# Prompt attention by pairs of heads, with weights normalised by GpSimd ahead of their transposes

## What is computed

```
def _fox_block(q, cq, q_pos, k, v, ck, k_pos):        # 8 heads of 64, cq and ck cumulated log-forget gates
    s = jnp.einsum('bqhd,bkhd->bhqk', q, k) * (HEAD_DIM ** -0.5)
    s = s + cq[..., :, None] - ck[..., None, :]
    s = jnp.where(k_pos[None, :] <= q_pos[:, None], s, -jnp.inf)
    p = jax.nn.softmax(s, axis=-1)
    return jnp.einsum('bhqk,bkhd->bqhd', p, v)
merged = jnp.concatenate([_rmsnorm(y_ssm, g_ssm_out), _rmsnorm(o, g_attn_out)], axis=-1)
out = merged @ w_out
```

## Time and profile before

| | us |
|---|---|
| runs | 2373.78, 2384.41, 2386.98 (median 2384.41) |
| profiled execution | 2372.85, its span 2371.1 |
| prompt attention | 529.2 to 759.3 |
| sample sequences | to about 902 |
| output projection | 902.9 to 1040.4 |

### The profile page before, as it was taken

How to read it: one execution, slowest core, us unless ns; L and a number is a source line. 1 busy time by engine, 2 the same in 40 slices (tenths; PEclk the granted TensorE clock), 3 DMA queues, 4 the chain that set the end, 5 groups by cost and what they waited for, 6 DMA issues and landing times.

```text
span 2371.1 us, 28991 instructions
## 1 busy us (share of the span) xinstructions
PE 2078.4 (88%) x8262; PEld 1117.0 (47%) x8263; DVE 892.5 (38%) x2450; ACT 533.7 (23%) x993; POOL 300.3 (13%) x236
## 2 busy tenths in 40 slices
PE   4797899998888888978978999899899999998990
PEld 1456555446666334545434444444445455544450
DVE  2827400315554222234423333333333333333338
ACT  3423221015544112033111111111111111111122
POOL 0010100000000030000001122122122222221124
PEclk7898889999998998988988999999899999999995
DMA  9531200022000443001148899899888778898843
GB/s 335 218 155 23 113 0 1 0 76 58 18 1 18 131 138 133 0 19 58 52 176 279 288 298 293 277 295 297 265 273 250 250 241 259 266 288 281 287 102 137
DMA packets 100878, 394.20 MB, mean 166 GB/s; under 512 B 27279, under 2 KB 30003, under 8 KB 71996
## 3 DMA queue, kind: packets, MB, share of 16 engines
q1 hardware_dynamic: 70020, 302.44, 34.4%
q0 software_dynamic: 24768, 90.19, 15.9%
q10 hardware_dynamic: 6024, 0.73, 0.2%
HBM read 329.16 MB, written 62.57 MB: 165 GB/s over the span
## 4 chain that ended last, share of the span: by engine, by line
PE 27%; DMA 22%; issue 5%; SPq 4%; DVE 2%; ACT 1%; POOL 0%; POOLq 0%; DVEq 0%; ACTq 0%
DMA arena<-in_w_exp_down 22%; PE psum L961 11%; PE psum L989 5%; PE psum L830 5%; SPq L2209 2%; PE psum L947 1%; SPq L2204 1%; SPq L2205 1%; DVE arena L1607 1%; PE psum L858 1%; PE psum L864 1%; DVE arena L1617 1%; PE psum L871 0%; PE psum L809 0%; PE psum L854 0%
## 5 line engine op out<-in xcount | busy, mean ns | idle before, releaser
L961 PE MATMUL psum<-arena 128*128 x1360 | 631.1, 619 | 55.2 <-SPq L2230 51.5
L961 PEld LDWEIGHTS psum<-arena 128*128 128x128 f32 x1360 | 261.1, 197 | 358.3 <-issue 358.3
L989 PE MATMUL psum<-arena,tail 128*128 x672 | 302.3, 592 | 0.0
L2057 POOL DMA_INDIRECT moe_rows<-arena x84 | 133.4, 1588 | 815.2 <-ACT arena L1941 291.4
L1563 DVE TENSOR_TENSOR arena<-arena,psum 128x256 f32<-128x256 f32 x85 | 35.8, 421 | 499.2 <-ACT arena L1927 499.2
L989 PEld LDWEIGHTS psum<-arena,tail 128*128 128x128 f32 x672 | 121.1, 190 | 120.5 <-issue 120.5
L1927 ACT ACTIVATE arena<-psum 128x256 f32<-128x256 f32 x85 | 32.7, 385 | 644.3 <-PE psum L961 644.3
L678 PE MATMUL psum<-arena 128*128 128x512 f32 (+1 forms) x384 | 126.5, 493 | 0.0
L830 PE MATMUL psum<-arena 128*128 128x512 f32 (+1 forms) x288 | 124.3, 593 | 0.9 <-ACT arena L1853 0.5
L1541 DVE TENSOR_TENSOR arena<-tail,arena 128x1152 bf16<-128x1152 f32 x89 | 119.6, 1344 | 0.0
L1941 ACT ACTIVATE arena<-psum,arena 128x512 f32<-128x512 f32 x84 | 57.7, 687 | 213.3 <-PE psum L989 213.3
(11 more groups left out here) (486 smaller groups left out, 2342.1 us busy)
## 6 DMA issues: line engine op xcount, KB each, us to landing
arena<-in_w_exp_gate SPq DMA_DIRECT2D x64, 1024.0 KB, 5.3
arena<-in_w_exp_up SPq DMA_DIRECT2D x64, 1024.0 KB, 9.4
arena<-in_w_exp_down SPq DMA_DIRECT2D x64, 1024.0 KB, 12.3
arena<-in_w_ada SPq DMA_DIRECT2D x24, 1024.0 KB, 7.6
arena<-in_w_ada_final SPq DMA_DIRECT2D x8, 1024.0 KB, 6.5
arena<-in_cache_k SPq DMA_DIRECT2D x32, 256.0 KB, 3.4
arena<-in_cache_v SPq DMA_DIRECT2D x32, 256.0 KB, 2.9
arena<-in_w_in SPq DMA_DIRECT2D x1, 6176.0 KB, 18.5
```

The costliest lines, as they stand in the source:

```text
L961: ins = pe.matmul(slot[2 + par].rearrange("p (h n) -> p h n", h=2), xTs[:, par, k, :], ring_gu[:, at, :, k, :].rearrange("p a h n -> p (a ...
L989: ins = pe.matmul(slot[1][:, n * 512:(n + 1) * 512], hTs[:, k, :], ring_d[:, at, k, n, :].rearrange("p a n -> p (a n)"), start=(k == 0), s ...
L2057: pool.indirect_dma_start(y_dram, bass.IndirectOffsetOnAxis(ap=s_idx[:, par:par + 1], axis=0), y_buf[:, par, :], None, compute_op=ALU.add) ...
```

## The change

Attention goes over 32 `PAIRS` of heads 2j and 2j+1 with the same query block, from i = 7 down to 0. `qT` holds the two heads of a pair on the two halves of the partitions. Both logits are matmuls of 64 rows, on the upper and the lower half of TensorE's rows, into slots 0 and 1. The causal mask is added by GpSimd into the diagonal block of `neg_c` before it is used (a block further right isn't needed again, as i falls). The exponentials stay in `sc`, which has four buffers; one over the sum is made, and GpSimd multiplies the weights with it in place. Then they are transposed. v is the stationary operand of the weighting, 64 columns for each head on one half of TensorE's columns, and the transposed weights move; the output comes out already transposed, in `oT`. Four spreads of 512 columns are made ahead and four in each of the first three rounds of eight pairs, into slot 4 or 5.

The norm's scale is applied by VectorE behind the projection's second half. Its squares are made by GpSimd right behind attention and summed by TensorE with eight one-column matmuls in the sample sequence b = 4; for the 64 sample rows ScalarE makes them as before, and only these rows are transposed there. SyncE loads the shared expert's weights when the last projection is done.

The diff, cut to its core:

```diff
@@ tiles
-        sc = arena(8192, 2, SEQ)
-        pr = arena(10240, 2, SEQ)
-        pt = arena(12288, 2, SEQ)
+        sc = arena(8192, 4, SEQ)
+        pt = arena(25888, 4, SEQ)
+        oT = arena(14336, KA, T)
-        ATT = [(i, h) for h in range(H) for i in range(8)]
+        PAIRS = [(i, j) for j in range(KA) for i in range(7, -1, -1)]
+        SPREAD_AT = (6, 5, 4, 3)
@@ TensorE
+            def logits(p):
+                i, j = PAIRS[p]
+                for a in range(2):
+                    fill(pe, ("L", 2 * p + a), a)
                 for c0 in range(0, (i + 1) * P, 512):
                     c1 = min(c0 + 512, (i + 1) * P)
+                    for a in range(2):
+                        h0, h1 = a * DH, (a + 1) * DH
+                        ins = pe.matmul(slot[a][:, c0:c1], qT[h0:h1, j, i * P:(i + 1) * P], kT[h0:h1, j, c0:c1], start=True, stop=True)
...
+            def turn_weights(p, a):
+                pe.wait_ge(pn_ready, it + 1)
...
+            def weigh(p):
+                fill(pe, ("O", p), 4 + p % 2)
+                for m in range(i + 1):
+                    for a in range(2):
...
+                        ins = pe.matmul(slot[4 + p % 2][a * DH:(a + 1) * DH, 0:P], v[:, m, (2 * j + a) * DH:(2 * j + a + 1) * DH],
+                                        pt[:, (2 * p + a) % 4, m * P:(m + 1) * P], start=(m == 0), stop=(m == i), skip_group_check=True)
+            logits(0)
+            for p in range(len(PAIRS)):
+                if p + 1 < len(PAIRS):
+                    logits(p + 1)
+                turn_weights(p, 0)
+                if p:
+                    weigh(p - 1)
+                turn_weights(p, 1)
+                if spread_of(p):
+                    spread_sums(*spread_of(p), 4 + (p + 1) % 2)
+            weigh(len(PAIRS) - 1)
...
+                if b == 4:
+                    pe.wait_ge(o_squares, 1)
+                    fill(pe, "OSS", 4)
+                    for t in range(8):
+                        ins = pe.matmul(slot[4][:, t:t + 1], o_acc.rearrange("p (c t) -> p t c", t=CH)[:, t], ones_col, start=True, stop=True)
@@ VectorE
+                for a in range(2):
+                    it = 2 * p + a
+                    full(dve, ("L", it))
+                    dve.wait_ge(c_masked, it + 1)
...
+                    if p:
+                        one_over_sum(it - 2)
+                for a in range(2):
+                    it = 2 * p + a
+                    slots.wait_empty(dve, ("L", it))
+                    dve.tensor_reduce(att_one[:, it % 4:it % 4 + 1], sc[:, it % 4, 0:n], AX.X, ALU.max, negate=True).then_inc(s_ready, 1)
...
-                ins = tt(mix, mix, slot[1][0:m, :], ALU.add)
+                ins = stt(mix, slot[1][0:m, :], rstd[0:m, t:t + 1], mix, ALU.mult, ALU.add)
@@ ScalarE
+            for p in range(len(PAIRS) + 1):
+                for a in range(2):
+                    if p < len(PAIRS):
+                        exponentials(2 * p + a)
+                    if p:
+                        weights_out(2 * p - 2 + a)
+                if p >= 2:
+                    attention_out(p - 2)
+                if p and spread_of(p - 1):
+                    spread_out(*spread_of(p - 1))
@@ GpSimd
-            pool.memset(qT[:, :, :], 0.0).then_inc(q_zero, 1)
+            def mask(p):
...
+                    diag = neg_c[h % 4][:, i * P:(i + 1) * P]
+                    pool.tensor_tensor(diag, diag, causal, ALU.add).then_inc(c_masked, 1)
+            def normalise(it):
+                n = (PAIRS[it // 2][0] + 1) * P
+                pool.wait_ge(recip_ready, it + 1)
+                pool.tensor_scalar(sc[:, it % 4, 0:n], sc[:, it % 4, 0:n], att_one[:, 8 + it % 4:9 + it % 4], None, ALU.mult).then_inc(pn_ready, 1)
+            for p in range(len(PAIRS) + 1):
+                if p < len(PAIRS):
+                    mask(p)
+                if p:
+                    normalise(2 * p - 2)
+                    normalise(2 * p - 1)
...
+            for n in range(2):
+                cols = slice(512 * n, 512 * (n + 1))
+                plink(pool.tensor_tensor(o_acc[:, cols], oT[:, 0, cols], oT[:, 0, cols], ALU.mult))
+                for j in range(1, KA):
+                    plink(pool.tensor_tensor(o_pow, oT[:, j, cols], oT[:, j, cols], ALU.mult))
+                    plink(pool.tensor_tensor(o_acc[:, cols], o_acc[:, cols], o_pow, ALU.add))
+            pool.sem_inc(o_squares, 1)
@@ SyncE
-            slots.wait_full(sp, ("OT", 8))
-            slots.wait_full(sp, ("OT", 7))
+            slots.wait_full(sp, ("W", NT - 1, 1))
             dma(sh_gu[:, :, 0:FE], ap["w_sh_gate"][0].rearrange("(k p) n -> p k n", p=P)).then_inc(ld_shared, 16)
```

More of the change, by code:

```diff
@@ L702, in _, with spread_sums @@
             full(ins, "LF")
[L704 to L710, removed]
+            def spread_sums(h, n, s_):
+                fill(pe, ("CB", h, n), s_)
+                full(pe.matmul(slot[s_], ident[0:H, h:h + 1].to_broadcast([H, P]), c_row[:, n * 512:(n + 1) * 512], start=True, stop=True), ("CB", h, n))
@@ L712, in _ @@
+            for i in range(4):
+                spread_sums(i // 2, i % 2, 4 + i % 2)
             slots.wait_empty(pe, ("V", 7))
-            def logits(it):
-                i, h = ATT[it]
-                fill(pe, ("L", it), it % 2)
+            def logits(p):
+                i, j = PAIRS[p]
+                for a in range(2):
+                    fill(pe, ("L", 2 * p + a), a)
                 for c0 in range(0, (i + 1) * P, 512):
                     c1 = min(c0 + 512, (i + 1) * P)
-                    ins = pe.matmul(slot[it % 2][:, c0:c1], qT[:, h, i * P:(i + 1) * P], kT[:, h // 2, c0:c1], start=True, stop=True)
-                full(ins, ("L", it))
@@ L722, in weigh @@
[L722 to L725, removed]
[L726 to L739 removed]
+                    for a in range(2):
+                        h0, h1 = a * DH, (a + 1) * DH
+                        ins = pe.matmul(slot[a][:, c0:c1], qT[h0:h1, j, i * P:(i + 1) * P], kT[h0:h1, j, c0:c1], start=True, stop=True)
+                        if c1 == (i + 1) * P:
+                            full(ins, ("L", 2 * p + a))
@@ L833, in _ @@
             project_out(0, 0)
[L835 to L842 removed]
+            slots.wait_empty(pe, "SR")
+            fill(pe, "OT", 2)
+            for k in range(KA):
+                ins = pe.transpose(slot[2][:, k * P:k * P + NS], o_smp[:, k * P:(k + 1) * P], ident[0:NS, 0:NS])
+            full(ins, "OT")
             for t in range(NT):
@@ L1381, in _ @@
             dlink(dve.reciprocal(rstd, rstd))
-            for t in range(NT):
-                ins = ts(o_tok[0:rows(t), t, :], o_tok[0:rows(t), t, :], rstd[0:rows(t), t:t + 1], None, ALU.mult)
-            dlink(ins)
-            dve.sem_inc(o_ready, 1)
             dve.wait_ge(ld_res, 32)
@@ L1818, in keys_out @@
                 if b == 0:
-                    full(act, ("O", len(ATT) - 1))
+                    full(act, ("O", len(PAIRS) - 1))
                 if b >= 2:
```

190 lines of the change are left out of this document (85 added, 105 removed).

## The result

The changed kernel takes 2445.9 us (median of 4 runs, 2440.8 to 2456.1), the kernel before 2379.6 beside it; the ratio is 1.028 (1.023 to 1.033). That is 66 us more, where 25 were forecast: the sign was right, the size was not, and 2445.9 lies outside of 2378 to 2442. The profiled execution has a span of 2439.0 us.

| us | before | changed | difference | forecast |
|---|---|---|---|---|
| attention | 233.7 | 315.1 | +81.4 | +35 |
| sample sequences | 143.8 | 158.3 | +14.5 | +3 |
| output projection | 137.5 | 125.6 | -11.9 | -12.7 |
| all behind it, unchanged | 1330.7 | 1314.1 | -16.6 | 0 |

The account below looks back on a forecast made before the run. Attention's new serial loop, with TensorE waiting on GpSimd's normalisation, was taken as the bound: 2372.85 + 35 (attention) + 3 (samples) - 12.7 (projection) = 2398, or 2410 as a median; range 2378 to 2442 (8 in 10).

Parts of the forecast that it names:

- the clock: Attention: share f at 1.2 GHz taken as 0.25, giving 265 us; ends 0.10 (251) and 0.45 (287).
- 242.5 / (1 - 0.34 f): Attention's length: 242.5 us at full clock, lengthened by the share f at 1.2 GHz, where a round takes 81.7, not 53.7.
- Rival 4: Attention: clock down half the time, or VectorE behind GpSimd; 287 plus up to 12 us, kernel 2425 to 2442; chance 0.17.
- Normalisation 2.85 us at 1024 columns: Attention: GpSimd's multiplication priced like the scaling of w_out, the dearest new term; 64 of them are 108 us.
- Rival 2: Attention: GpSimd normalises faster, deciding from 1.7 us at k = 8; 2369, 0.6% faster; 0.12 with anything shortening the loop.
- Halves side by side: Attention: row-half logits and column-half weighting run beside each other on TensorE, 0.058 us per instruction.
- Rival 3: Attention: the halves don't run beside each other; kernel 2472, or about 2440 with the weighting alone in series; chance 0.04.
- The serial turn: Attention: logits, sum, reciprocal, two normalisations, transposes, next logits in sequence; 9.8 us per turn at k = 8.
- Spreads: Attention: TensorE waits for ScalarE's copies before spreading the cumulated gates; 2.3 us in 12 places, 27.6.
- VectorE beside GpSimd in attention: Attention: VectorE's sums slowed by GpSimd, taken as nothing, at most 10 us.
- Sample part: Sample sequences: VectorE's short operations behind GpSimd's squares cost 0 to 15 us, 3 taken; one-column matmuls taken as 0.
- Projection: Output projection: squares, root, scaling and 36 transposes leave the path, 12.7 us gained; x1 and shared weights hidden.

Follow-up runs that it names:

- changed, again: The changed kernel run once more with no edit: ratio 1.032 (1.028 to 1.036) to the kernel before, attention 312.4 us.
- half filled: Changed kernel plus unneeded TensorE multiplications of 96 columns per key block in its wait for the first normalised weights: 2419.8 us, ratio 1.022.
- filled: Changed kernel plus unneeded TensorE multiplications of 192 columns per key block in its wait for the first normalised weights: 2400.5 us, ratio 1.012.
- The early reciprocal: Changed kernel with VectorE making each reciprocal before the next pair's logit sum instead of behind it: 2364.4 us, ratio 0.999, attention 239.0 us.

## Why the prediction was right in sign and wrong in size

**The step that failed is the clock.** The working took f, the share of attention at 1.2 GHz, as 0.25 with 0.45 as the upper end; it was 0.66. The rest of that step held: 242.5 / (1 - 0.34 f), counted from the first logits, against four stretches measured from there:

| kernel | f | formula | measured |
|---|---|---|---|
| changed | 0.66 | 312.7 | 307.8 |
| changed, again | 0.66 | 312.7 | 305.1 |
| half filled | 0.44 | 285.2 | 284.1 |
| filled | 0.20 | 260.2 | 262.8 |

So the turns, their prices and what a microsecond at 1.2 GHz costs were, as a sum, right within 3%, and one number accounts for the miss: with f = 0.66 in place of 0.25 the formula goes from 265 to 312.7 us, 48 more, of which the stretch kept 43 (307.8 less 265). Attention was missed by 46. (The other 3.5 are a term that was left out: the changed kernel makes four spreads ahead of its first logits, 7.3 us, where the kernel before needed 3.8 for this place.) Rival 4 had the mechanism, but stopped at half the time and had 0.17. Its sum also has a slip: 287 us is what the formula gives at f = 0.45, not at half the time; with f = 0.5 it is 292, and with the 12 us for VectorE the top of the range would have been about 2449. That would have held 2445.9, but partly by luck: in attention no wait of VectorE ended with GpSimd.

What misled was the earlier trace rows: a stretch in which TensorE was busy for 12.1 of 13.6 us, and that stayed at 0.50, was read as "work of little streaming doesn't bring the clock back", and the 512-column logits of the new loop as the remedy. What TensorE would do between its pieces got no price. By the forecast's own terms it had 108 us of work at 2.4 GHz (288 blocks of 0.11 + 0.115 + 0.115, and 24 instructions of 0.43) in 242.5 us. Two stretches of the kernel before in which TensorE also waits again and again are the beginning of the program and a part of the state-space group; the prediction did not look at them. Windows of the kernel before, columns as above, the first row split in two by the next two:

```profile
0.00:59.30 59.30, 26.82 (x125) 9.06 (x126) 16.60 (x87) 18.36 (x30) 3.82 (x21) 0.71 0.93 335
...
0.00:20.00 20.00, 6.11 (x34) 2.28 (x35) 1.17 (x6) 4.64 (x6) 2.63 (x18) 1.00 0.70 263
20.00:59.30 39.30, 20.71 (x91) 6.78 (x91) 15.43 (x81) 13.72 (x24) 1.19 (x3) 0.56 1.05 372
...
200.00:260.00 60.00, 37.30 (x501) 33.58 (x497) 46.99 (x92) 18.46 (x51) 0.00 (x0) 0.78 0.05 7
```

The first row's 0.71 is f = 0.58, which gives a stretch of 302 us and a sum of 2447. That this is so near to the measured time is chance: 0.71 is the mean of 20 us at 1.00 and 39 at 0.56, and by these 39 us f would be 0.88 and the stretch 346 us. By the last row f is 0.44 and the stretch 285. So rows with much waiting would have widened the range to both sides of what was measured; they would not have given 0.66. All this was worked out afterwards.

Waiting is not all that takes the clock, and how it follows from the work stays open. In the earlier trace rows TensorE waited for only 1.5 of 13.6 us at 0.50. In the samples of the changed kernel the clock falls while TensorE works without a pause, among the one-column matmuls:

```profile
926.00:927.70 1.70, 1.70 (x15) 0.94 (x14) 0.65 (x3) 0.00 (x0) 0.00 (x0) 1.00 0.77 167
927.70:929.70 2.00, 2.00 (x9) 1.92 (x9) 1.25 (x3) 0.64 (x2) 0.00 (x0) 0.99 0.80 245
929.70:931.70 2.00, 2.00 (x10) 2.00 (x11) 0.00 (x0) 0.18 (x2) 0.00 (x0) 0.50 0.90 308
```

**Point by point.**

- Normalisation 2.85 us at 1024 columns: 2845 ns, 109.6 us for all 64 (108 forecast). Rival 2 is gone, by its own point of decision. The Trainium skill's page "GPSIMD Engine Reference", Engine selection, has one-input operations on GpSimd roughly at line rate; the traces disagree, 2.85 us against VectorE's 0.98 for the same operation on the same memory.
- Halves side by side, 0.058 each: 0.0625 and 1.35 us for 1.38. Rival 3 is gone.
- The serial turn: right. Waits of 4.2 us in the long turns (about 4 forecast), ended by GpSimd. The early reciprocal shows that its place behind the sum made the chain, 76 us by the traces, the clock's share in it included.
- Spreads, 2.3 us in 12 places: at 563.2 the transposes end, at 565.18 the logits start, 2.0.
- VectorE beside GpSimd in attention, taken as nothing: right, 1275 ns for a sum of 1024 columns.
- Sample part, +3 with 0 to 15: 14.5, at the end of the range. 5.0 are VectorE's short operations beside the squares (3.1 of it the eight copies), where 3 were taken. The one-column matmuls, taken as hidden, are the other term that was mis-sized: TensorE had no wait in b = 4 that could cover them, 3.8 us. The clock was lower there too, 0.84 against 0.91; that it makes up the 5.7 us that remain was not tested by itself.
- Projection, -12.7: -11.9. x1 and the shared weights were hidden as worked out (first use at 1149.91, 25 us after the projection's end).
- Unchanged part: 16.6 us shorter. In the trace of before some 14 of them lie between 1484 and 1720 us, at a clock of 0.93; all other traces of this part are shorter than its 1330.7, from 1298 to 1324. Whether that is the one execution or an effect of what runs before it stays open. Between these two traces it hides a part of the miss.

## What to carry to other kernels

When an edit makes TensorE wait in every turn of a loop, price the loop at both clocks, and let the range of the lower one's share take in every stretch of the old trace in which TensorE waits again and again: here these gave 0.44 to 0.88, the forecast went to 0.45 only, and the share was worth 43 us. Before an operation is made cheaper, ask behind what it stands: moving a reciprocal of 0.15 us in an engine's queue was worth 76 us, making the multiplication behind it three times as fast 13 to 16. And after each move look at the next queue, since what ScalarE's order cost, 40 us with the spreads, could not be seen as long as GpSimd was later.

## What the runs showed of the hardware that was not expected

- Work without a purpose can shorten a kernel: 26 thousand columns of additional multiplications took 45 us off attention, as the granted clock went from 0.66 to 0.89, and the ratio to the kernel before went from 1.028 (1.032 when run again) to 1.012.
- A one-column matmul whose stationary operand is every eighth column of a tile started every 0.238 us, with weight loads of 334 ns, at a granted clock of 1.00 and of 0.50 alike. One-column matmuls with the columns side by side (L664 of the changed kernel) started every 0.112 us.
- Some of VectorE's operations from SBUF to SBUF with one input tensor slowed down beside GpSimd's two-input ones (copies of 64 columns from 0.20 to 0.60 us, and back to 0.20 with the squares moved away; an operation on 8 columns from 0.22 to 1.12), while its sums from PSUM with one SBUF tensor did not (1275 ns beside GpSimd's multiplication). The Trainium skill's page "GPSIMD Engine Reference", Specifications, names contention for VectorE's two-port modes and for two SBUF inputs; by that rule the sums, which have one input in SBUF, do not contend, and the trace agrees (1275 ns). Whether the copies ran in a two-port mode no run shows.
- VectorE multiplied 1024 columns of fp32 by a scalar per partition in 978 ns, GpSimd in 2845.
